# Last 16 of 32 experts: gate and up products of all of them first, then down weights by blocks of 512 columns, with the per-layer gate's contraction block by block behind

## The reference, cut to what matters

```python
def channel_mix(x, p_i, ...):
    x = x + hier_moe(rmsnorm(x, g_ffn), ...)      # each token: 2 of 32 experts, weighted sum
    # expert e:  (silu(xb @ w_gate[e]) * (xb @ w_up[e])) @ w_down[e]
    #            w_gate, w_up: 2048 x 512,  w_down: 512 x 2048
    # then: x = x + sigmoid(rmsnorm(x, g_ple) @ w_ple_gate) * (p_i @ w_ple_proj)
    #            w_ple_gate: 2048 x 2048, w_ple_proj: 256 x 2048
# at the end: y = rmsnorm(x, g_final)
```

## Time and profile before

| what | value |
|---|---|
| median of 3 runs | 1596.82 us (1596.01 to 1597.22) |
| profiled execution | the page gives its span, 1598.9 us from the first to the last instruction, and no further time of its own |
| TensorE busy | 1393.6 us, 87% |
| VectorE, ScalarE, GpSimd busy | 368.2, 272.1, 39.0 us |
| chain that ended last | DMA 39%, TensorE 30% |
| read from HBM | 510 MB |

### The profile page before, as it was taken

How to read it: one execution, slowest core, us unless ns; L and a number is a source line. 1 busy time by engine, 2 the same in 40 slices (tenths; PEclk the granted TensorE clock), 3 DMA queues, 4 the chain that set the end, 5 groups by cost and what they waited for, 6 DMA issues and landing times.

```text
span 1598.9 us, 21909 instructions
## 1 busy us (share of the span) xinstructions
PE 1393.6 (87%) x9232; PEld 777.3 (49%) x9233; DVE 368.2 (23%) x933; ACT 272.1 (17%) x584; POOL 39.0 (2%) x82
## 2 busy tenths in 40 slices
PE   9999999999999998778868887868769769688997
PEld 7878888888877443223223233323223223233543
DVE  3312231045612213012012012112112112122212
ACT  3102121132211311110111111101101101113203
POOL 1000000020040010000000000000000000000000
PEclk9999999999999899897999999989989989999999
DMA  9556333469987999999999999999999999995342
GB/s 309 184 161 200 122 131 121 146 237 329 345 299 295 359 405 428 427 428 428 428 429 428 427 427 428 428 426 428 429 428 429 429 427 429 428 427 197 122 170 80
DMA packets 101359, 527.39 MB, mean 330 GB/s; under 512 B 12342, under 2 KB 34814, under 8 KB 74910
## 3 DMA queue, kind: packets, MB, share of 16 engines
q1 hardware_dynamic: 98014, 525.18, 81.9%
q10 hardware_dynamic: 3272, 1.15, 0.3%
HBM read 509.99 MB, written 16.23 MB: 329 GB/s over the span
## 4 chain that ended last, share of the span: by engine, by line
DMA 39%; PE 30%; DVE 1%; ACT 1%; issue 1%; ACTq 0%; SPq 0%; DVEq 0%
DMA more<-in_w_up 24%; DMA raw<-in_w_up 8%; PE ps L1963 8%; PE ps L2213 7%; DMA raw<-in_w_gate 5%; PE ps L155 4%; PE ps L1273 3%; PE ps L1984 2%; PE ps L1213 2%; DMA more<-in_w_down 2%; PE ps L1972 1%; PE ps L1938 1%; PE ps L2230 1%; PE ps L1277 0%; PE ps L1495 0%
## 5 line engine op out<-in xcount | busy, mean ns | idle before, releaser
L1963 PE MATMUL ps<-raw,hT 128*32 128x512 f32 x1488 | 204.3, 683 | 113.2 <-DMA raw<-in_w_gate 59.5
L155 PE MATMUL ps<-hT,raw 128*128 128x264 f32 x1280 | 292.8, 388 | 0.0
L155 PEld LDWEIGHTS ps<-hT,raw 128*128 128x128 f32 x1280 | 241.8, 191 | 42.4 <-issue 1.7
L1963 PEld LDWEIGHTS ps<-raw,hT 128*32 128x32 f32 x1488 | 44.3, 117 | 244.1 <-issue 85.3
L155 PE MATMUL ps<-mixT,raw 128*128 128x264 f32 x640 | 146.6, 390 | 2.7 <-PEq L837 1.7
L155 PEld LDWEIGHTS ps<-mixT,raw 128*128 128x128 f32 x640 | 121.9, 192 | 25.9 <-issue 4.2
L1984 PE MATMUL ps<-more,hid 128*32 128x512 f32 x992 | 118.6, 611 | 13.3 <-DMA more<-in_w_down 13.3
L1874 DVE TENSOR_TENSOR hid<-ps,sig 128x128 f32<-128x128 f32 x32 | 9.3, 291 | 487.2 <-PE ps L1972 487.2
L1972 PEld LDWEIGHTS ps<-fold,hT 128*128 128x128 f32 x512 | 70.9, 211 | 100.7 <-ACT hT L1806 63.9
L2213 PE MATMUL ps<-raw,more 128*128 128x512 f32 x256 | 112.3, 594 | 0.0
L1963 PE MATMUL ps<-more,hT 128*32 128x512 f32 x512 | 84.9, 796 | 25.8 <-DMA more<-in_w_up 25.8
(11 more groups left out here) (408 smaller groups left out, 889.9 us busy)
## 6 DMA issues: line engine op xcount, KB each, us to landing
more<-in_w_down SPq DMA_DIRECT2D x64, 2048.0 KB, 25.7
raw<-in_w_gate SPq DMA_DIRECT2D x62, 2048.0 KB, 25.9
more<-in_w_up SPq DMA_DIRECT2D x32, 2048.0 KB, 25.9
raw<-in_w_up SPq DMA_DIRECT2D x31, 2048.0 KB, 26.3
raw<-in_w_in SPq DMA_DIRECT2D x44, 1024.0 KB, 5.1
raw<-in_w_out SPq DMA_DIRECT2D x16, 1024.0 KB, 10.8
raw<-in_w_ple_gate SPq DMA_DIRECT2D x16, 1024.0 KB, 5.0
x_res<-in_state_mlstm_C SPq DMA_DIRECT2D x8, 1024.0 KB, 8.4
```

The costliest lines, as they stand in the source:

```text
L155: return nc.tensor.matmul(ps[:, j, 0:NT], core.raw[:, q % NCH, k * GW + j * P:k * GW + (j + 1) * P], xT[:, core.groups[g].k0 + c * CK + k, ...
L1963: last = nc.tensor.matmul(ps[own, (GATE, UP)[m], :], xT[:, k, i * SLOTS:(i + 1) * SLOTS], weights, start=(i == 0 and k < 4), stop=(i == EI ...
```

## The change: what it does, and the diff

- Experts 0 to 15 run as before. For experts 16 to 31 (`LATE`) only gate and up are loaded and computed (`load_late`, `late`), in the ring's first four places. Each one's hidden rows stay in `late_h`, and the chosen rows of each four in `late_rowsT`.
- Then `finish_stage` goes through four blocks of 512 columns. For a block `g` it loads the 512 columns of `w_down` of all 16 experts (1 MB each, eight places, waited for in pairs), and for each four experts (a group, `j`) runs `down`, a copy by ACT and `sums`, which adds the four groups up in PSUM.
- Behind it, in block `g + 1`, the finished 512 columns of `x` are transposed and multiplied by their 512 rows of `w_ple_gate` (`gates`), for all 2048 output columns; DVE adds the partial results up in `pre`. Block 3's part follows the last group.
- The pieces of `w_ple_gate` are 512 x 512 as before, now by row blocks, in places of their own. SP issues them among the down loads, each behind a wait for the matmuls that used its place.
- Only then come the roots, the sigmoids, the final norm and the stores. `last_down`, `last_rows` and the handling apart of the last expert are gone, and so are the second loads after further passes.

```diff
+FULL = 16
+LATE = NE - FULL
+BLOCKS = D // GW
+PLACES = 8
...
+            def load_late(e, used):
+                for at in range(2 * EI):
+                    sp.wait_ge(q["chunk_used"], used + (at + 1))
+                    item(e, at)
...
+            def late(i):
+                for q4 in range(4):
+                    e = i * 4 + q4
+                    pe.wait_ge(q["x_copied"], e + 1)
+                    project(0, 0, e)
+                    project(0, 1, e)
+                    project(1, 0, e)
+                    pe.wait_ge(q["late_ready"], e - (FULL - 1))
+                    folded(0, e, False)
+                    gather_slots(core, pe, rt, q, e + 1)
+                    if q4 == 3:
+                        late_rows_turn(core, pe, q, i)
+                    project(1, 1, e)
+                    x_turn(e + 1)
+                    folded(1, e, False)
...
+def load_gate(core, w, sp, g, n, landed):
+    src = weight_group(w["w_ple_gate"][0], slice(n * GW, (n + 1) * GW))[:, g * CK:(g + 1) * CK, :]
+    sp.dma_start(weight_piece(core, n).rearrange("p (k c) -> p k c", k=CK), src).then_inc(landed, 16)
...
     def sync(sp):
+        def down(g, l):
+            pair = g * LATE // 2 + l // 2
+            if l % 2 == 0:
+                if pair < PLACES // 2:
+                    sp.wait_ge(shared["chunk_used"], (FULL + 1) * ECH + (LATE - 1) * 2 * EI + pair + 1)
+                else:
+                    sp.wait_ge(q["down_done"], pair // 2 - 1)
+            src = w["w_down"][0, FULL + l].rearrange("(k p) c -> p k c", p=P)[:, :, g * GW:(g + 1) * GW]
+            sp.dma_start(place(l).rearrange("p (k c) -> p k c", k=4), src).then_inc(pair_landed[pair % (PLACES // 2)], 16)
+        def piece(g, n):
+            if g:
+                sp.wait_ge(q["gate_done"], 3 * (4 * (g - 1) + n + 1))
...
+        for n in range(4):
+            piece(0, n)
+        for g in range(BLOCKS):
+            for j in range(GROUPS):
+                for l in range(4 * j, 4 * j + 4):
+                    down(g, l)
+                if g >= 2 and j < 2:
+                    piece(g - 1, j + 2)
+                if 1 <= g < LAST and j >= 2:
+                    piece(g, j - 2)
+                if (g, j) == (1, 0):
+                    gains()
+        for n in range(4):
+            piece(LAST, n)
...
     def tensor(pe):
+        def down(g, j):
+            n = g * GROUPS + j
+            for pair in (2 * n, 2 * n + 1):
+                pe.wait_ge(pair_landed[pair % (PLACES // 2)], 32 * (pair // (PLACES // 2) + 1))
+            if n >= 2:
+                pe.wait_ge(q["y_taken"], n - 1)
+            for k in range(4):
+                for i in range(4):
+                    l = 4 * j + i
+                    last = nc.tensor.matmul(ps[i * SLOTS:(i + 1) * SLOTS, Y_BANKS[n % 2], :], late_h[:, 4 * l + k, :],
+                                            place(l)[:, k * GW:(k + 1) * GW], start=(k == 0), stop=(k == 3))
+            last.then_inc(q["down_done"], 1)
...
+        for g in range(BLOCKS):
+            for j in range(GROUPS):
+                if g == LAST and j:
+                    gates(g - 1, j)
+                down(g, j)
+                if g and j == 0:
+                    turn(g - 1)
+                if g and (g < LAST or j == 0):
+                    if j == 0:
+                        sums(g, j)
+                    gates(g - 1, j)
+                if not (g and j == 0):
+                    sums(g, j)
+        turn(LAST)
+        for n in range(4):
...
+            gate_tile(T0, LAST, n, last_bank[T0, n])
+            if n == 1:
+                total(part_s, 1, q["t_part"], 0)
...
+        for i, (kind, n) in enumerate(items):
...
+            dve.wait_ge(q["gate_done"], 3 * 4 * LAST + i + 1)
+            V.tensor_tensor(dst, src, dst, ALU.add).then_inc(q["logit_ready"], 1)
+            if i:
+                weigh(i - 1)
+            dve.wait_ge(q["gate_ready"], i + 1)
+            link(V.tensor_tensor(gate[i % 3], gate[i % 3], p, ALU.mult))
+            V.tensor_tensor(row, row, gate[i % 3], ALU.add).then_inc(q["x_updated"], 1)
+            if i == 5:
+                scale(T0)
+            if i == 7:
+                scale(SMP)
```

More of the change, by code:

```diff
@@ L2143, in tail_stage @@
     tile = {T0: 0, T1: 1}
[L2144 to L2150 removed]
+    KINDS = (T0, T1, SMP)
+    GROUPS = LATE // 4
+    Y_BANKS, SUM_BANK, GATE_BANK = (0, 1), {T0: 2, T1: 3, SMP: 4}, {T0: 5, T1: 6, SMP: 7}
+    LAST = BLOCKS - 1
+    items = [(T0, n) for n in range(4)] + [(SMP, 0)] + [(T1, n) for n in range(4)]
@@ L2259, in total @@
-        def total(source, count, bank):
-            pe.wait_ge(q["t_squared"], count)
-            nc.tensor.matmul(ps[:, bank, 0:1], tail["same"][:], source, start=True, stop=True
-                             ).then_inc(q["t_total"], 1)
-        last_rows(0)
-        turn(0)
-        turn(1)
-        last_rows(1)
-        prompt(0, 0, 0)
-        turn(2)
-        prompt(0, 0, 1)
-        turn(3)
-        last_samples()
-        prompt(0, 0, 2)
-        turn(4)
-        prompt(0, 0, 3)
-        turn(5)
@@ new lines, in sums @@
+        def sums(g, j):
+            n = g * GROUPS + j
+            pe.wait_ge(q["y_taken"], n + 1)
+            if j == 0 and g:
+                pe.wait_ge(q["x_added"], 3 * g)
+            y = bounce[n % 2]
+            for t, kind in ((0, T0), (1, T1)):
+                ins = nc.tensor.matmul(ps[:, SUM_BANK[kind], :], late_rowsT[:, j, t * P:(t + 1) * P], y, start=(j == 0), stop=(j == GROUPS - 1))
+                if j == GROUPS - 1:
+                    ins.then_inc(q["block_ready"], 1)
+            for a in range(4):
+                last = nc.tensor.matmul(ps[a * SLOTS:(a + 1) * SLOTS, SUM_BANK[SMP], 0:P], late_rowsT[:, j, SEQ:SEQ + SLOTS],
+                                        y[:, a * P:(a + 1) * P], start=(j == 0), stop=(j == GROUPS - 1))
+            last.then_inc(q["sums_done"], 1)
@@ new lines, in gates, with total @@
+        def gates(g, n):
+            pe.wait_ge(piece_landed[n], landed_before + 16 * (g + 1))
+            for i, kind in enumerate((T0, T1)):
+                if n == 0:
+                    rows_ready(kind, g)
+                else:
+                    pe.wait_ge(q["gate_taken"], TAKEN * g + 2 * (n - 1) + i + 1)
+                gate_tile(kind, g, n, GATE_BANK[kind])
+            if n == 0:
+                rows_ready(SMP, g)
+            gate_samples(g, n).then_inc(q["gate_done"], 1)
+        def total(source, count, sem, col):
+            pe.wait_ge(sem, count)
+            nc.tensor.matmul(ps[:, SUM_BANK[SMP], col:col + 1], tail["same"][:], source, start=True, stop=True
+                             ).then_inc(q["t_total"], 1)
```

753 lines of the change are left out of this document (353 added, 400 removed).

## The result

The changed kernel takes 1586.99 us (median of four, 1584.81 to 1589.01), the kernel before beside it 1597.02 (median of four, 1596.01 to 1598.15). The ratio is 0.9928, with a 95% interval of 0.991 to 0.9946: faster by 10 us. The forecast was 1573, faster by 24. The range, 1558 to 1592, holds the result; the gain is less than half of the one forecast.

A forecast was written before the change was run, and what follows sets the result against it. Transfers bound the experts, TensorE the last stretch, serially. Gate and up in at 1288.0, plus 65.7 and 2.4 to 1356.1, plus 167.4 of TensorE to 1523.5, end 1575.2, less 2.1: 1573 us; range 1558 to 1592.

The forecast's parts named there:

- Up to expert 15 nothing moves: Stretch up to expert 15: no time gained or lost by the change.
- Gate and up: Experts 16 to 31: transfers set the pace, 19.6 us per expert, done at 1288.0; the four-place ring costs nothing.
- Block 0, 2-KB packets at 383: Block 0's loads, 25.2 MB in 2-KB rows at 383 GB/s: 65.7 us, group (1,0) in at 1356.1.
- So TensorE becomes the bound: Blocks 1 to 3: TensorE needs 167.4 us, transfers 156, so TensorE sets the pace by a narrow margin.
- the clock rival: Blocks: TensorE's clock falls after waits, twelve groups lose 1.5 us each, + 18, so 1591 us; 14%.
- 80.7 MB of the rivals: Bytes from 1288.0 to the last group, used for the hidden rival (1543 us, 5%) and starved rival (1635 us, 9%).
- SP's queue, cost nothing: Blocks: SP, issuing in order, is held up to 12 us behind gate pieces; loads in flight cover it, cost nothing.
- TensorE's clock in blocks 1 to 3: Blocks 1 to 3: the forecast charged no clock loss; a down group of 5 us would show it wrong.
- The starved stream: Blocks: down loads held behind gate pieces run nearly one by one, at 280 GB/s 1635 us, slower; 9%.
- the hidden case: Blocks: TensorE keeps up and all its work hides under transfers at 410 GB/s, 1543 us; 5%.
- The end: After the last sums at 1523.5: last gate block, nine items mostly 2.9 us apart, stores; end at 1575.2.
- From span to median: Whole run: 2.1 us taken off the summed end of 1575.2, the profiled span being that far above the median.

The follow-up runs named there:

- the samples' run: Changed kernel with only one of four contraction rows computed for the samples' gate work in blocks 0 to 2: 1579.01 us, ratio 0.986 to the kernel before.
- Moving the input: Changed kernel with the projected per-layer input made beside experts 8 to 11, not 12 to 15: 1580.4 us, ratio 0.9871 to the kernel before.
- the same move in the old order: Kernel before, with the projected per-layer input made beside experts 8 to 11: 1604.0 us, ratio 1.0032 to the unedited kernel before.
- wide rows: Changed kernel with down loads of experts 16 to 31 as 128 rows of 8 KB, same bytes: 1580.93 us, ratio 0.99 to the kernel before.
- the warm matmuls: Changed kernel with four unused matmul calls behind each group of block 0, to keep TensorE's clock up: 1584.06 us in one execution.
- the bridge alone: Changed kernel with block 0's four gate pieces issued right behind expert 16's loads: 1588.72 us, ratio 0.9912; repeated 1584.32 us, 0.9904, to the kernel before.
- bridge and earlier input: Changed kernel with block 0's gate pieces behind expert 16's loads and the projected input beside experts 8 to 11: 1579.42 us, ratio 0.9884 to before.

## Why the prediction was right in sign and wrong in size

I set the profile after against the prediction's points, all of them on the profiled executions' clocks.

*"Up to expert 15 nothing moves."* Right of the code, and yet 4.0 us came from there. The issue that is the 97th expert load stands at 949.9 us before and at 945.9 after. TensorE's gather of one expert, L1213 before, L1217 after, begins at nearly the same time in both; before:

```profile
548.81 5.50 PE L1213 MATMUL ps<-x_res,mine 128*32 128x512 f32 x24
```

and after:

```profile
548.50 2.92 PE L1217 MATMUL ps<-x_res,mine 128*32 128x512 f32 x24
```

In the window 550 to 560 us the granted clock is 0.61 before and 1.00 after. The profiled execution of before had a stretch at the lower level in it. Such a gather comes later in both (736.47 us before, 821.61 after), but there the transfers kept their pace, 428 GB/s from 600 to 940 us in both; from 540 to 600 us they moved 399 GB/s before and 421 after, 3.1 us of transfers. That a stretch of like code can differ so much shows in the new order too: from the first expert load to the 97th it takes 483.4 us in the profile of the result and 487.6 in that of the samples' run, whose code is the same up to there; before took 487.5. So of the 15.8 us between the spans (1598.9 and 1583.1) 4.0 are not the change's, and 11.8 are, where the sum said 23.7.

*Gate and up, "so I cost it at nothing".* This is the step that failed: "The ring now has four 2-MB places, not six; with one in use three are still in flight, 14.7 us of transfers, so I cost it at nothing." It holds from expert to expert: TensorE's projections behind a wait start at 1112.85, 1132.43 and 1152.01 us in its chain, 19.6 apart, as forecast. I did not ask it of the one place where the rhythm breaks, the passage from expert 15 to 16. No place comes free for 28 us there, and the four places hold 19.6 us of transfers, the three that I counted 14.7. From the 97th issue to the end of the 16-KB stream I had 338.1 us; it took 345.7. These 7.6 us are the 7.4 of the gap. Moving the input took the gap away, the same move in the old order did not pay, and both repeats of the changed kernel have the gap.

*Block 0, 2-KB packets at 383.* Right: they ran at 387, and wide rows gained 3.5 us, so the price is the packets'. Stream end to block 1's start was 67.3 us, 68.1 forecast. The Trainium skill (DMA: Bandwidth & Descriptors, Specifications) gives 512 B as the size from which a transfer runs at line rate. The runs go on disagreeing with it: 387 GB/s for rows of 2 KB, 416 for 8 KB, 428 for 16 KB.

*"So TensorE becomes the bound."* Right in kind: leaving out three quarters of the samples' work in three blocks took 7.8 us off the same stretch, and a faster stream took none but the first product's. The size was off by 5.0, 172.4 where I had 167.4. This is the second step that was mis-sized. Of the 5.0, 1.9 are the first product, which runs at a lower granted clock after block 0's waits (5.34, while 3.43 is the steady one); the clock rival had priced this, but for all twelve groups, and the forecast for none. With the warm matmuls it took 3.64, so 1.7 of them came back. The rest is the group: 13.78 for my 13.47, which is 3.7 for twelve; the transposes (1.13 for 1.3) and each block's first sums (2.08 for the steady 2.27) give 1.1 of it back, and block 3 takes 0.5 more than I had. The down product is shorter than I took (3.43 for 3.57), the quarter of the gate longer (8.07 for 7.83), and the sums with it (2.27 for 2.07).

The sum for the transfers beside it has a slip. For block 3 up to its last group I put 18.9 MB, but SP's program issues three groups and two gate pieces there, 14.7 MB or 38 us at 383. Only this makes up the 80.7 MB of the rivals (25.2, 19.9, 21.0 and 14.7). So the transfers needed 145 us and not 156, and the margin by which TensorE is the bound was 22 us and not 11. The choice of the bound stands, and the time is not touched.

*SP's queue, cost nothing.* Right. The wait of SP shows in the 214 GB/s at 1480 to 1500 us, and TensorE's chain has no gap there. *TensorE's clock in blocks 1 to 3:* whole, but for the one product. The starved stream did not come, nor the hidden case.

*The end.* From the last sums I had 51.7 us, and it took 51.8. The items, ACT's and SP's timeline after:

```profile
1545.22 0.63 ACT L2365 ACTIVATE early<-oT 128x512 f32<-128x512 f32 x1 [1.48 <-DVE oT L2499]
...
1556.51 0.63 ACT L2365 ACTIVATE early<-early 128x512 f32<-128x512 f32 x1 [1.48 <-DVE early L2499]
...
1560.07 1.28 ACT L2374 ACT_TABLE_LOAD   x1
1562.96 1.28 ACT L2394 ACT_TABLE_LOAD   x1
...
1566.47 0.63 ACT L2365 ACTIVATE early<-oT 128x512 f32<-128x512 f32 x1 [1.48 <-DVE oT L2499]
...
1575.08 0.63 ACT L2365 ACTIVATE early<-oT 128x512 f32<-128x512 f32 x1 [1.49 <-DVE oT L2499]
...
1578.73 0.81 SPq L2228 DMA_DIRECT2D out_y_prompt<-x_res  x2
```

The items are counted from 0 here, as in the forecast, whose "first of nine" is item 0. The squares of items 0 to 4 lie 2.8 us apart (1545.22 to 1556.51 is four steps), 2.9 forecast; item 6 (1566.47) has its two table loads ahead of it and comes 7.1 after item 5 (7.0 forecast), and item 8 (1575.08) follows item 7 after 5.8 (5.6).

*From span to median.* I took 2.1 off, as before's profiled execution stood 2.1 above its median. After, the median lies 3.9 above the profiled span. That is 6.0 the other way, the same chance as in the first point. On record every execution takes about 1.7 us longer than its span (1584.81 for 1583.1), so after's profiled execution was 2.2 faster than its median; before's, whose own time is not on record, was by the same 1.7 an estimated 3.8 slower.

Together: 7.6 for the ring, -0.8 for block 0, 5.0 for the blocks and 0.1 for the end are 11.9. Less 4.0 by chance, and 6.0 for the median, makes 13.9 of the 14.0 between 1573 and 1586.99. So 12 of the 14 us have a cause in the kernel, and 2 are chance.

That the range, 1558 to 1592, held the result was partly luck. Its upper side was meant for waits at each of twelve groups and for a slow clock in the blocks. Of that came one slow product, 1.9 us; the largest part, the ring's 7.6, had no term in it.

## What to carry to other kernels

A ring of fewer places must be asked about at the rhythm's breaks, not in its rhythm: find the longest time for which the consumer frees nothing, and count the bytes in flight at its start. Loads that a change takes away may have been the ones that bridged it. And where single runs differ by several us, compare the stages inside the profiles from one fixed event to the next.

## What the runs showed of the hardware

- In the two runs with the bridge alone, TensorE stood for 3.6 and 3.8 us after the third record of the blocks' first product, where no semaphore is waited for; with bridge and earlier input it did not. No experiment tried to tell why; a packet on an instruction queue came 2.3 to 2.9 us before it went on.
- In the changed kernel SP spent 15.6 us on its first six down issues (1 MB each, rows of 2 KB, from 1293.4 us); with rows of 8 KB it spent 5.8. The three profiles with the bridge, all with rows of 2 KB, have 11.6 to 16.0. More rows hold SP longer; whether their number alone does it, no run tells.
- One expert's gather took 5.50 us in one execution and 2.92 in another, at the same point of the same code; the granted clock over it was 0.50 and 1.00. Slow gathers come later too, at 736 us in the one and at 821 in the other, and there they cost no transfer time (428 GB/s from 600 to 940 us in both).
